# The opening of a fused mLSTM/Hyena layer on one core: modulation products in column tiles, token turns behind products, two high halves on VectorE, gate columns in two products

## The reference, cut to what matters

```python
s_lat = silu(c);  s_ctx = silu(c_ctx)
shift_l, scale_l, gate_l = split(s_lat @ w_mod + b_mod, 3)      # w_mod: 1024 x 3072
shift_c, scale_c, gate_c = split(s_ctx @ w_mod + b_mod, 3)
hl = rms_norm(xl, pre_gain) * (1 + scale_l) + shift_l
hc = rms_norm(xc, pre_gain) * (1 + scale_c) + shift_c
qk, v, o, zm, g, hy, zh = split_proj(h @ w_in)                  # g: 16 gate columns (4 kinds x 4 heads)
```

## Time and profile before

| | us |
|---|---|
| median of three runs | 1611.21 (1604.7 to 1611.88) |
| the profiled execution | 1611.5, of which the span is 1609.7 |
| PE busy | 1553.9 (97%) |
| PEld, DVE, ACT, POOL busy | 1352.4, 688.9, 635.3, 306.6 |
| first projection product starts | 52.28 |
| tile 4 starts | 70.36 |
| gate tiles | 166.58 to 191.2 |

### The profile page before, as it was taken

How to read it: one execution, slowest core, us unless ns; L and a number is a source line. 1 busy time by engine, 2 the same in 40 slices (tenths; PEclk the granted TensorE clock), 3 DMA queues, 4 the chain that set the end, 5 groups by cost and what they waited for, 6 DMA issues and landing times. The chain is left out here.

```text
span 1609.7 us, 23024 instructions
## 1 busy us (share of the span) xinstructions
PE 1553.9 (97%) x8916; PEld 1352.4 (84%) x8916; DVE 688.9 (43%) x1122; ACT 635.3 (39%) x1359; POOL 306.6 (19%) x297
## 2 busy tenths in 40 slices
PE   8799999999999999999999999999999888999997
PEld 3688888888888888888888899999999787888886
DVE  1654420233333332201020277777775567555553
ACT  2885311333222222113111255545454275555451
POOL 1552000000000000000000021111213125665662
PEclk9899999999999999999999999999999999999999
DMA  9332521222222111312122455655545584666651
GB/s 358 99 115 66 190 99 48 84 72 79 72 78 72 72 59 64 105 46 99 53 76 72 168 164 135 183 135 146 140 92 157 187 257 149 199 194 194 199 183 53
DMA packets 127940, 201.77 MB, mean 125 GB/s; under 512 B 12523, under 2 KB 75457, under 8 KB 120934
## 3 DMA queue, kind: packets, MB, share of 16 engines
q1 hardware_dynamic: 127846, 200.49, 39.4%
HBM read 122.42 MB, written 52.86 MB: 109 GB/s over the span
## 5 line engine op out<-in xcount | busy, mean ns | idle before, releaser
L502 PE MATMUL bank<-h_hi,w_hi 128*128 128x512 f32 (+1 forms) x840 | 324.8, 387 | 0.0
L504 PE MATMUL bank<-h_hi,w_lo 128*128 128x512 f32 (+1 forms) x840 | 323.1, 385 | 0.0
L503 PE MATMUL bank<-h_lo,w_hi 128*128 128x512 f32 (+1 forms) x840 | 322.9, 384 | 0.0
L502 PEld LDWEIGHTS bank<-h_hi,w_hi 128*128 128x128 f32 x840 | 158.4, 189 | 31.2 <-issue 0.2
L504 PEld LDWEIGHTS bank<-h_hi,w_lo 128*128 128x128 f32 x840 | 158.2, 188 | 31.2
L503 PEld LDWEIGHTS bank<-h_lo,w_hi 128*128 128x128 f32 x840 | 158.3, 188 | 31.0 <-issue 0.2
L878 DVE SCALAR_TENSOR_TENSOR work<-work,coef 128x504 f32<-128x504 f32 (+1 forms) x84 | 62.3, 742 | 239.8 <-ACT work L658 239.8
L502 PE MATMUL bank<-w_hi,h_hi 128*128 128x512 f32 (+1 forms) x448 | 164.5, 367 | 0.0
L503 PE MATMUL bank<-w_lo,h_hi 128*128 128x512 f32 (+1 forms) x448 | 164.1, 366 | 0.0
L504 PE MATMUL bank<-w_hi,h_lo 128*128 128x512 f32 (+1 forms) x448 | 164.1, 366 | 0.0
L648 ACT ACTIVATE work<-bank 128x512 f32<-128x512 f32 (+1 forms) x72 | 40.4, 562 | 296.7 <-PE bank L504 296.7
(11 more groups left out here) (237 smaller groups left out, 2768.1 us busy)
## 6 DMA issues: line engine op xcount, KB each, us to landing
H<-spectrum SPq DMA_DIRECT2D x192, 128.0 KB, 2.3
stage<-in_w_in SPq DMA_DIRECT2D x18, 1024.0 KB, 5.7
s_hy<-work SPq DMA_DIRECT2D x48, 256.0 KB, 2.2
x<-s_hy SPq DMA_DIRECT2D x8, 1024.0 KB, 5.6
kq<-s_k SPq DMA_DIRECT2D x32, 256.0 KB, 4.7
v<-s_v SPq DMA_DIRECT2D x32, 256.0 KB, 5.0
mb<-s_rows SPq DMA_DIRECT2D x32, 256.0 KB, 5.7
late<-in_x SPq DMA_DIRECT2D x16, 512.0 KB, 5.0
```

The lines of the kernel that those rows point to most:

```text
L502: pe.matmul(out, lhs[0], rhs[0], start=(k == 0), stop=False)
L503: pe.matmul(out, lhs[0], rhs[1], start=False, stop=False)
L504: return pe.matmul(out, lhs[1], rhs[0], start=False, stop=(k == KD - 1))
```

## The change

1. The modulation products of k go to four column tiles of 32: k and k + 4 accumulate in PSUM rows 32(k mod 4) and up. `svec` is written into a 32-column block with zeros (`svec_wide`), and all 128 rows of a bank are copied. The turn is a product of the copied rows with `quarters` (128 x 2), which adds up the four quarters.
2. `ident` is loaded second, and silu waits for it. `turn_mod(1)` stays after piece 4, `turn_mod(2)` moves from piece 6 to after piece 7, before `turn_mod(3)`. `turn(2)` and `turn(3)` move behind tile 0, and behind tile n (from 1 on) stands `turn(n + 3)`.
3. `high(0)` and `high(1)` move from ACT to VectorE, `low(0)` from VectorE to POOL; the splits of the two first weight pieces move behind the first two blocks, on ACT and VectorE; `normalise` and `square` change places with them as below.
4. SP loads blocks 2 and 3 before the second piece of w_in.
5. The `w_lo` of the gate columns gets the high halves again in its columns 0 to 3 of each kind and the low halves in columns 8 to 11, so that a gate tile takes two products for each k in place of three. The gate rows come back as eight transfers, and VectorE adds them (`join_rows`).

```diff
-GATE_LOADS = {G0 + 2: 1, V0: 2, V0 + 4: 3}
+GATE_LOADS = {G0 + 2: 1, V0 + 2: 2, V0 + 4: 3}
-GATE_SUMS, TURN_ROWS = {V0 + 2: (0, 1), V0 + 8: (2, 3)}, V0 + 14
+GATE_SUMS, TURN_ROWS = {V0 + 4: (0, 1), V0 + 8: (2, 3)}, V0 + 14
+        svec_wide = hidden[:, 0:KD * QUARTER].rearrange("p (k m) -> p k m", k=KD)
+        quarters = hidden[:, KD * QUARTER:KD * QUARTER + 2]
+        def turned_behind(n):
+            return (2, 3) if n == 0 else range(n + 3, min(n + 4, NT))
 # sync
-            sp.dma_start(cvec[:, :, :], d["cvec"]).then_inc(cvec_in, 16)
+            sp.dma_start(cvec[:, :, :], d["cvec"]).then_inc(first_in, 16)
+            sp.dma_start(ident[:, :], d["ident"]).then_inc(first_in, 16)
...
-            for par in range(2):
-                sp.wait_ge(mod_used, par + 1)
-                sp.dma_start(stage[:, par, :, :], d["w_in"][par]).then_inc(w_loaded[par], 16)
+            sp.wait_ge(mod_used, 1)
+            sp.dma_start(stage[:, 0, :, :], d["w_in"][0]).then_inc(w_loaded[0], 16)
             for j in range(2, 4):
                 sp.wait_ge(xt_ready, j - 1)
                 load_x(j)
+            sp.wait_ge(mod_used, 2)
+            sp.dma_start(stage[:, 1, :, :], d["w_in"][1]).then_inc(w_loaded[1], 16)
...
-                        for dst, kind in ((ipre, 0), (fpre, 1)):
-                            r0 = 32 * (2 * dr + kind)
+                        for dst, kind, row in ((ipre, 0, 0), (fpre, 1, 0), (bsum, 0, LOW_ROW), (logf, 1, LOW_ROW)):
+                            r0 = 32 * (2 * dr + kind) + row
 # tensor
+                pe.wait_ge(svec_ready, 4)
                 for i in range(4):
-                    mm = pe.transpose(psM[:, 4 * row + i, :], modrow[row % 2][:, i * P:(i + 1) * P], ident[0:2, 0:2])
+                    mm = pe.matmul(psM[:, 4 * row + i, :], modrow[row % 2][:, i * P:(i + 1) * P], quarters,
+                                   start=True, stop=True)
...
-                    mm = pe.matmul(bank[c // 2][0:2, c % 2 * SLOT:(c % 2 + 1) * SLOT], svec[:, k, :],
-                                   mod_weights(c)[:, k, :], start=(k == 0), stop=(k == KD - 1))
+                    at = k % 4 * QUARTER
+                    mm = pe.matmul(bank[c // 2][at:at + QUARTER, c % 2 * SLOT:(c % 2 + 1) * SLOT], svec_wide[:, k, :],
+                                   mod_weights(c)[:, k, :], start=(k < 4), stop=(k >= 4))
...
-                if c in (2, 4, 6):
+                if c in (2, 4):
                     turn_mod(c // 2 - 1)
+            turn_mod(2)
             turn_mod(3)
-            turn(2)
-            turn(3)
...
-                if n + 4 < NT:
-                    turn(n + 4)
+                for j in turned_behind(n):
+                    turn(j)
...
-                channels_tile(n % 4, 0, 0, t0, width)
+                out = bank[n % 4][:, 0:width]
+                for k in range(KD):
+                    pe.matmul(out, w_lo[:, 0, k, 0:P], h_hi[:, k, t0:t0 + width], start=(k == 0), stop=False)
+                    mm = pe.matmul(out, w_hi[:, 0, k, 0:P], h_lo[:, k, t0:t0 + width], start=False, stop=(k == KD - 1))
+                mm.then_inc(tile_ready, 1)
 # scalar: the order
-            take_mod(0); take_mod(1); split(0, 0, 1, None); take_mod(2); split(1, 1, 1, None)
-            square(2); square(3); take_mod(3)
-            modulate(0); high(0); modulate(1); high(1); square(4)
-            modulate(2); high(2); modulate(3); high(3); square(5)
+            take_mod(0); take_mod(1); take_mod(2); take_mod(3)
+            modulate(0); modulate(1); split(0, 0, 1, None); square(2); square(3)
+            split(1, 1, 1, None); square(4); square(5)
+            modulate(2); high(2); modulate(3); high(3)
             for n in range(K_TILES + 2):     # modulate and high of n + 3 from n = 1 on, square of n + 5
 # gpsimd: the order
-            root(0) to root(3); root(4); low(2); root(5); low(3)
+            root(0); root(1); low(0); root(2) to root(5); low(2); low(3)
 # vector
+            def split_gate():
+                by_kind = lambda t, par, first: t[:, par, :, 0:P].rearrange("p k (g j) -> p k g j", g=4)\
+                    [:, :, :, first:first + HEADS]
...
+                dve.tensor_copy(by_kind(w_lo, 0, 0), by_kind(w_hi, 0, 0))
+                dve.tensor_tensor(by_kind(w_lo, 0, LOW_ROW), by_kind(stage, 0, 0), by_kind(w_hi, 0, 0).bitcast(F32),
+                                  ALU.subtract).then_inc(w_lo_ready, 1)
-            normalise(0); normalise(1); split(0, 0, None); split(1, 1, None); mod and gcol
-            modulate(0); modulate(1); low(0); low(1); normalise(2); normalise(3)
-            modulate(2); normalise(4); modulate(3)
+            normalise(0); normalise(1); quarters; mod and gcol
+            modulate(0); high(0); modulate(1); high(1); low(1); split(0, 0, None)
+            normalise(2); normalise(3); split(1, 1, None); normalise(4); modulate(2); normalise(5); modulate(3)
...
+            def join_rows():
+                dve.wait_ge(rows_in, 128)
+                dve.tensor_tensor(fpre, fpre, logf, ALU.add).then_inc(rows_set, 1)
+                dve.tensor_tensor(ipre, ipre, bsum, ALU.add).then_inc(rows_set, 1)
...
             accumulate_gate(0)
+            split(4, 0, V0)
             accumulate_gate(1)
-            split(4, 0, V0)
+            join_rows()
```

More of the change, by code:

```diff
@@ L183, in project @@
         gcol = sb("gcol", [P, KD, 2])
-        modrow = [work[0:2, 2 * D + i * TILE:2 * D + (i + 1) * TILE] for i in range(2)]
+        modrow = [work[:, 2 * D + i * TILE:2 * D + (i + 1) * TILE] for i in range(2)]
+        svec_wide = hidden[:, 0:KD * QUARTER].rearrange("p (k m) -> p k m", k=KD)
+        quarters = hidden[:, KD * QUARTER:KD * QUARTER + 2]
         second = sb("second", [P, D])
@@ L307, in _ @@
                     for dst, src in ((bmod[:, :], d["bmod"]), (pgain[:, :], d["pgain"]), (gbias[:, :], d["gbias"]),
-                                     (coef[:, :, :], d["coef"]), (ident[:, :], d["ident"])):
+                                     (coef[:, :, :], d["coef"])):
                         sp.dma_start(dst, src).then_inc(small_loaded, 16)
-            for par in range(2):
-                sp.wait_ge(mod_used, par + 1)
-                sp.dma_start(stage[:, par, :, :], d["w_in"][par]).then_inc(w_loaded[par], 16)
+            sp.wait_ge(mod_used, 1)
+            sp.dma_start(stage[:, 0, :, :], d["w_in"][0]).then_inc(w_loaded[0], 16)
             for j in range(2, 4):
@@ L673, in take_mod @@
                     act.wait_ge(mod_turned, row - 1)
-                act.copy(modrow[row % 2], bank[row][0:2, :]).then_inc(mod_rows, 1)
+                act.copy(modrow[row % 2], bank[row][:, :]).then_inc(mod_rows, 1)
             square(0)
             square(1)
-            take_mod(0)
-            take_mod(1)
+            for row in range(4):
+                take_mod(row)
+            modulate(0)
+            modulate(1)
             split(0, 0, 1, None)
-            take_mod(2)
-            split(1, 1, 1, None)
             square(2)
             square(3)
[L685 to L688, removed]
+            split(1, 1, 1, None)
             square(4)
-            for j in range(2, 4):
-                modulate(j)
-                high(j)
             square(5)
+            modulate(2)
+            high(2)
+            modulate(3)
+            high(3)
             for n in range(K_TILES + 2):
-                if n + 4 < NT:
-                    modulate(n + 4)
+                if 1 <= n and n + 3 < NT:
+                    modulate(n + 3)
                 if n >= 2:
                     conv_end((n - 2) % 4, n - 2, k_tile(n - 2)[2])
[L699 to L702, removed]
+                if 1 <= n and n + 3 < NT:
+                    high(n + 3)
+                if 1 <= n and n + 5 < NT:
+                    square(n + 5)
                 if n < K_TILES:
@@ L809, in _ @@
             pool.wait_ge(power_set, 2)
-            for j in range(4):
+            root(0)
+            root(1)
+            low(0)
+            for j in range(2, 6):
                 root(j)
-            root(4)
             low(2)
-            root(5)
             low(3)
@@ L868, in low, with high @@
                    .then_inc(lo_ready, 1)
+            def high(j):
+                dve.wait_ge(ht_act, j + 1)
+                dve.wait_ge(ht_dve, j + 1)
+                dve.tensor_copy(h_hi[:, :, bass.ts(j, P)], ht[j % 2]).then_inc(hi_ready, 1)
             def taps(n, slot, c, r, width, blk, rows):
@@ L884, in _ @@
             modulate(0)
+            high(0)
             modulate(1)
-            low(0)
+            high(1)
             low(1)
+            split(0, 0, None)
             normalise(2)
             normalise(3)
+            split(1, 1, None)
+            normalise(4)
             modulate(2)
-            normalise(4)
+            normalise(5)
             modulate(3)
             for n in range(K_TILES + 1):
-                if n + 4 < NT:
-                    modulate(n + 4)
```

(8 more changed lines are left out.)

30 lines of the change are left out of this document (19 added, 11 removed).

## The result

| | before | changed |
|---|---|---|
| median of 10 runs (range) | 1609.49 us (1604.7 to 1611.88) | 1597.13 us (1593.51 to 1606.01) |
| profiled execution, span | 1611.5, 1609.7 | 1599.17, 1597.4 |
| start of `modulate(0)`, the hinge M | 41.91 | 34.95 |
| tile 0 | 52.28 | 43.73 |
| tile 4 | 70.36 | 65.31 |

The changed kernel takes 0.9927 of the time before, 95% interval 0.9911 to 0.9943: 11.7 us faster, where 12.2 were forecast against the median of three runs. In the profiled executions the span is 12.3 us shorter. The stage told of here ends at about 900 us; what comes behind it, the same in all kernels, took between 692 and 701 us in the 13 profiled executions of this document. So a few us are read from where a stage starts and ends, and not from the span of one profile.

The account below looks back on a forecast made before the run. TensorE, busy for 97% of the span, was taken to bound the kernel. Hinge earlier -7.9, new order's cost +3.6 and gate tiles -8.2 gave -12.5 us: 1599, own range 1596 to 1603, stated range 1594 to 1608.5.

Parts of the forecast that it names:

- (a): Opening, modulation products and turns: column tiles and new order bring M from 41.91 to 34.0, 7.9 us earlier.
- records start in order: Modulation products: the second record of k overlaps only the first of k + 1, so 9 slots, 1.99 us a piece.
- four wide: Rival on the modulation products: four column tiles run side by side all the time, -1.1 us, 1598; chance 0.15.
- a slow clock in piece 7 +2.0: Range width in the opening: the last modulation piece runs at a slow clock, costing 2.0 us more.
- four side by side, -1.1: Range width in the opening: four column tiles' records run together, 1.1 us less than forecast.
- (b): From M to tile 4: the new order starts tile 0 at M + 9.3, tile 4 at M + 31.1, costing 3.6 us.
- the list of signs: The prediction's closing list of what would show it, including PE waiting some 2.5 us for tile 4.
- Cover of tiles 8, 12 and 16: Projection behind tile 4: blocks turned one tile before have cover 0.6, costed at nothing; at most 0.4 three times.
- (c): Gate tiles: a third of the products goes, saving 8.2 us, with cover of 0.7 behind them as before.
- the gate tiles give nothing back: Rival: v tiles wait for rows, weights or stores timed by the gate tiles; up to 8.2 lost, 1607; chance 0.06.
- Tiles in a row: Rival on the modulation products: records of different column tiles don't overlap, PE stays late, 1607.7; chance 0.20.
- The weight load no longer hides: Rival on the modulation products: loads into another column tile wait, each record costs 0.379, total 1628; chance 0.06.

Follow-up runs that it names:

- the second profile: The changed kernel, unaltered, timed and profiled again beside the kernels with filler: 1599.37 us, ratio 0.9940.
- the two runs on the layout: The changed kernel with modulation products in two column tiles, 1597.79 us, and with neighbours k and k + 1 in the same one of four tiles, 1596.37 us.
- the lighter filler: The changed kernel plus unread products in the opening's waits, before `turn(6)` and before tile 4, fewer behind the pieces than in the other fillers: 1594.20 us, ratio 0.9907.
- the gate part alone: The kernel before with only the gate part (two products per k, eight row transfers, later splits and sums): 1602.46 us, ratio 0.9960.
- The opening alone: The changed kernel with the gate part undone: 1607.53 us, ratio 0.9997.

## Why the prediction was right, step by step

The count of the gate tiles was right for its reason. The opening came out right partly by luck: two terms of (a) were wrong in opposite directions, and a fall of the clock at tile 4, which no term has, was absent from the profile that the sum is checked on.

**(a) The hinge: right in direction, its largest term mis-sized.** Predicted 7.9 earlier, measured 7.0 (6.2 in the second profile, where piece 7 starts 0.7 later). The piece landed at 28.55 where I had 29.35. The burst, 1.99 by "records start in order", is 1.07 at full clock: that reason was wrong, four wide was the true rival, as the two runs on the layout show. By itself it would have put M at about 32.5 (28.55 + 1.00 until the first turn + 2.90 from there to M, both from the lighter filler, at full clock). What took the gain back is what I had only as a width of the range ("a slow clock in piece 7 +2.0"): the burst took 1.87 up to the first turn in place of 1.00, and from there to M it was 4.53 in place of 2.90 (the turns 3.58 in place of 1.95): 0.9 and 1.6, together 2.5 us. I also took 0.85 for a turn on eight wide transposes; at full clock two turns are 1.94 to 1.95. So "four side by side, -1.1" and "slow clock, +2.0" both came, and that the sum stayed near is luck. (The widths of the prediction's own range add up to 1597 to 1603.5, not 1596 to 1603.) The Trainium skill, page TensorEngine Tiling (Array Packing), section Key Properties, has tiles that load and multiply in parallel; the measured bursts agree, with 1.07 for what took 3.54. No row bears out the order-bound version that I preferred to it.

**(b) M to tile 4: right within 0.8 in the first profile, its price short by 2.0 in the second.** Tile 0 at M + 8.78 (9.3), its half-clock stretch 5.2 us long (4.9), the copy behind POOL's difference as predicted, ACT's queue without a gap from 50.02 to 62.7, tile 4 at M + 30.36 (31.1). PE waited 1.21 before `turn(6)` and 1.79 before tile 4, 3.0 in all; the working had 3.9 and the list of signs 2.5. Its price of 3.6 comes out as 3.3: the first gate tile is 3.67 earlier than before, which is 7.0 less 3.3. In the changed kernel's second profile it is 5.6 (M 6.2 earlier, the first gate tile 0.7): tile 4 is at M + 31.05, and the half clock behind it costs 1.6. The prediction has no term for that fall, and eight of the nine profiles with the new order and no filler there have it. Cover of tiles 8, 12 and 16: PE waits 0.2 us in all from 66 to 300 us, before tile 16. That cover was thinner than 0.6, and cost nothing else.

**(c) The gate tiles: exact.** 8.2 predicted; 24.62 less 16.44 is 8.18. The cover behind them was 0.7 by my sum and is 0.75 measured: the rival "the gate tiles give nothing back" is refuted here and in the gate part alone, where the stage end moved by the same 8.2. The eight transfers of the rows (187.76, 3.32 us long) end long before ACT wants them.

**The other rivals.** Tiles in a row: refuted, eight bursts in place of gapless products. The weight load no longer hides: refuted, a record in a burst costs 0.07 and not over 0.25. The run without column tiles comes near what the first would have looked like: M at 41.1 and not 42.7, since its small turns take 0.40 each where the prediction had 0.85, and the stage end 7.6 later.

**The sum.** -7.0 + 3.3 - 8.2 = -11.9 up to V0 (191.2 to 179.35), -11.5 at the stage end, -12.3 in the span. The last 0.8 is less than the part behind the stage differs by from one execution to the next. In the second profile the stage end is only 8.5 earlier, and the median of its six runs, 1599.37, is a ratio of 0.9940 or 9.7 us. Both medians lie near the forecast of 1599. With its fall of the clock at tile 4 the second profile is the more usual of the two.

**What stays open.** The opening alone has no time that tells it from nothing, only a trace. That the clock falls because PE idles between bursts rests on filling those gaps, which kept it up in all three kernels that did, and on the longer bursts of two tiles. When it falls is not settled: in all six profiles with four tiles and no filler it fell, in four of them too late to be back for piece 7 and the turns (M 34.95 to 35.8), in two at about 22 us, early enough (M 32.5 and 33.3). So the 2.5 us of slow clock are not paid in every execution, and how often they are the profiles are too few to tell.

## What to carry to other kernels

Before making a product cheaper in a stretch that transfers pace, ask what the freed time turns into: here it became idle time, then a lower clock for the turns and the tile that the whole kernel was waiting for. Some 5 us of gain lay there and in a second fall of the clock behind two short waits, to be had with products that nobody reads. When two errors of opposite sign are both written down as widths, price them together, since the one (a shorter burst) brings the other (idle, so a slower clock). A count of products taken from a stretch where TensorE never waits (the gate tiles) is worth its face value, if the cover of what follows is measured from the end of that stretch.

## What the runs showed of the hardware that was not expected

- Column tiles of 32 take their records independently of the order in which these are issued: 16 records of 256 columns in 1.07 us with four tiles, 1.09 with neighbours in the same tile, 1.92 with two. The Trainium skill, page TensorE: Matmul & The Clock Gate, section What overlaps and what doesn't, calls products first in, first out in start and end; within one tile that may hold, across tiles the run with neighbours in one tile speaks against it.
- TensorE's granted clock fell from 1.00 to 0.50 while bursts of 1.07 us came every 2.5 us, in all six such profiles; with bursts of 1.92 and in the kernels with filler it did not (1.00 from 28 to 34 us). Later it fell around the waits before and behind one turn (1.2 and 1.8 us in the changed kernel's first profile, which kept its clock), in eight profiles of nine (0.72 from 66 to 72 us in one of the changed kernel, 1.00 in the other).
- VectorE and POOL hold each other up both ways. VectorE's copy of 128 x 1024 takes 0.69 alone and 1.60 beside POOL's difference (2.36); POOL's power of 128 x 1, 0.55 alone, takes 2.48 beside VectorE's split of 2.28 (41.55, above).
- The burst between 6 and 10 us took 1.94 us, as it does at half clock, while the profile shows 1.00 there. The clock's record in this trace begins only at 14.7 us, so its first rows are to be read by the distance of the records.

```profile
6.00:10.00 4.00, 1.94 (x16) 0.69 (x16) 0.00 (x0) 1.90 (x3) 0.62 (x2) 1.00 1.02 418
```
